# The filter taps as two rounded products over 128 stacked rows in place of one plain product

## The reference, cut to what matters

```python
z = jnp.concatenate([t, jnp.cos(bands * ang), -jnp.sin(bands * ang)], axis=-1)   # 1024 x 33
hid = jnp.sin(fr1 * (z @ w1 + b1))                                               # 1024 x 64
hid = jnp.sin(fr2 * (hid @ w2 + b2))                                             # 1024 x 64
filt = (hid @ w3).reshape(L, HYENA_ORDER, FILTER_DIRS, D_HYENA)                  # 1024 x 2048
filt = filt * jnp.exp(-t * jnp.abs(deltas))[:, None, None, :]
fwd, bwd = filt[:, :, 0], jnp.flip(filt[1:, :, 1], axis=0)
```

## Time and profile before

| | |
|---|---|
| median of 3 runs | 3659.33 us (3657.73 to 3661.23) |
| the profiled execution | 3661.77 us, its span 3660.0 us |
| mean granted clock of TensorE | 0.963 |
| TensorE busy | 3364.4 us (92%), 15224 instructions |
| VectorE busy | 1764.8 us (48%) |
| ScalarE busy | 1115.5 us (30%) |
| GpSimd busy | 579.7 us (16%) |
| the stage of the change | from about 237 to 427 us of the span |

### The profile page before, as it was taken

The page is one execution under the profiler, slowest core; times in us unless marked ns, Lnnn a source line. Parts: engine busy times, 40 slices in busy tenths (PEclk is TensorE's granted clock), DMA queues, the critical chain, the costliest instruction groups (busy, mean ns, idle before and its releaser), DMA issues. The chain is left out here.

```text
span 3660.0 us, 39794 instructions
## 1 busy us (share of the span) xinstructions
PE 3364.4 (92%) x15224; PEld 2696.9 (74%) x15224; DVE 1764.8 (48%) x2726; ACT 1115.5 (30%) x1955; POOL 579.7 (16%) x401
## 2 busy tenths in 40 slices
PE   7999888876989899999999998988899899999998
PEld 5776666665777587888888776776666688888886
DVE  4425544457341435555554539789543423242334
ACT  4323333325232322122111424136675321111212
POOL 0002365642100001010000200000164201000010
PEclk8999999988999999999999999999999999999999
DMA  4232323230321004332221301123233111111111
GB/s 122 75 101 84 118 78 115 87 134 15 117 68 65 37 20 133 98 97 97 97 80 48 133 18 41 46 56 84 67 67 114 39 58 47 46 52 50 47 46 58
DMA packets 223493, 270.27 MB, mean 74 GB/s; under 512 B 17259, under 2 KB 150276, under 8 KB 221298
## 3 DMA queue, kind: packets, MB, share of 16 engines
q1 hardware_dynamic: 223348, 268.30, 23.6%
HBM read 219.68 MB, written 29.18 MB: 68 GB/s over the span
## 5 line engine op out<-in xcount | busy, mean ns | idle before, releaser
L193 PE MATMUL psum<-rounded,rounded 128*128 128x512 f32 (+2 forms) x3936 | 1540.7, 391 | 115.6 <-DVE rounded L222 51.3
L194 PE MATMUL psum<-rounded,rounded 128*128 128x512 f32 (+2 forms) x3936 | 1530.5, 389 | 0.0
L195 PE MATMUL psum<-rounded,rounded 128*128 128x512 f32 (+2 forms) x3936 | 1529.1, 388 | 0.0
L193 PEld LDWEIGHTS psum<-rounded,rounded 128*128 128x128 f32 x3936 | 748.1, 190 | 293.1 <-DVE rounded L222 56.5
L195 PEld LDWEIGHTS psum<-rounded,rounded 128*128 128x128 f32 x3936 | 747.7, 190 | 152.4
L194 PEld LDWEIGHTS psum<-rounded,rounded 128*128 128x128 f32 x3936 | 749.0, 190 | 148.8 <-issue 0.2
L2966 DVE TENSOR_TENSOR plain<-psum,plain 128x512 f32<-128x512 f32 x432 | 288.2, 686 | 110.7 <-PE psum L195 109.1
L2977 DVE TENSOR_TENSOR plain<-psum,plain 128x512 f32<-128x512 f32 x44 | 30.4, 691 | 424.1 <-ACT plain L2881 424.1
L3538 POOL TENSOR_TENSOR plain<-plain,plain 128x128 f32<-128x128 f32 (+3 forms) x64 | 96.9, 1523 | 591.4 <-ACT plain L3636 516.0
L3343 DVE TENSOR_SCALAR_CACHE_REDUCE plain<-plain,plain 128x384 bf16<-128x384 f32 (+2 forms) x204 | 181.8, 942 | 1.3
L2958 DVE TENSOR_TENSOR rounded<-plain,rounded 128x512 fp32r<-128x512 f32 x108 | 97.2, 900 | 164.8 <-ACT rounded L2870 164.6
(11 more groups left out here) (327 smaller groups left out, 3467.1 us busy)
## 6 DMA issues: line engine op xcount, KB each, us to landing
plain<-in_ff_w_dram SPq DMA_DIRECT2D x64, 512.0 KB, 5.4
plain<-in_w_ada_dram SPq DMA_DIRECT2D x96, 256.0 KB, 3.3
plain<-in_w_gu_dram SPq DMA_DIRECT2D x44, 512.0 KB, 4.9
plain<-in_w_in_dram SPq DMA_DIRECT2D x36, 512.0 KB, 4.0
rounded<-rounded SPq DMA_DIRECT2D x72, 256.0 KB, 3.4
plain<-in_c_fwd_dram SPq DMA_DIRECT2D x64, 256.0 KB, 2.6
plain<-in_w_down_dram SPq DMA_DIRECT2D x22, 512.0 KB, 3.7
fold<-plain SPq DMA_DIRECT2D x8, 1024.0 KB, 5.0
```

The costliest lines, as they stand in the source:

```text
L193: nc.tensor.matmul(out, wh, xh, start=first, stop=False)
L194: nc.tensor.matmul(out, wh, xl, start=False, stop=False)
L195: return nc.tensor.matmul(out, wl, xh, start=False, stop=last)
```

## The change

The hidden values are made twice: `w2`, the bias and the frequency are loaded into both halves of the partitions, so that the second hidden layer gives the same 64 channels on partitions 0 to 63 and 64 to 127. A tile `stack` then holds the rounded part of the hidden values in rows 0 to 63 and, after a subtraction, the rest in rows 64 to 127. `w3` is loaded twice too, and `w3_hi` holds its rounded part in all 128 rows, `w3_lo` its rest in 64. A product over the 128 rows gives hi x hi + lo x hi, a second one over 64 rows adds hi x lo. So each plain product becomes two rounded ones.

```diff
-        self.loads = [(self.z, core.ap["c_z"]), (self.w1, core.ap["hy_filt_w1"][0]), (self.w2, core.ap["hy_filt_w2"][0])]
-        for i, name in enumerate(("hy_filt_b1", "hy_filt_freq1", "hy_filt_b2", "hy_filt_freq2")):
-            self.loads.append((self.vec[:, i:i + 1], core.ap[name].rearrange("a c -> c a")))
+        self.loads = [(self.z, core.ap["c_z"]), (self.w1, core.ap["hy_filt_w1"][0])]
+        for part in range(2):
+            rows = slice(64 * part, 64 * part + 64)
+            self.loads.append((self.w2[:, rows], core.ap["hy_filt_w2"][0]))
+            for i, name in enumerate(("hy_filt_b1", "hy_filt_freq1", "hy_filt_b2", "hy_filt_freq2")):
+                self.loads.append((self.vec[rows, i:i + 1], core.ap[name].rearrange("a c -> c a")))
...
     def next_taps(self, sp):
         S = self.core.sig
         sp.wait_ge(S["tap_done"].sem, S["tap_done"].at(8))
-        sp.dma_start(self.w3, self.core.ap["hy_filt_w3"][0][:, L:2 * L]).then_inc(S["taps_loaded"].sem, 16)
+        for rows in (slice(0, 64), slice(64, P)):
+            sp.dma_start(self.w3[rows, :], self.core.ap["hy_filt_w3"][0][:, L:2 * L]).then_inc(S["taps_loaded"].sem, 16)
...
-            last = nc.tensor.matmul(ps[0:64, 6 + half, :], w, x[:, half * BANK:(half + 1) * BANK], start=True, stop=True)
+            last = nc.tensor.matmul(ps[0:64 * (layer + 1), 6 + half, :], w, x[:, half * BANK:(half + 1) * BANK], start=True, stop=True)
...
+    def high(self, act):
+
+        S = self.core.sig
+        act.wait_ge(S["sine_done"].sem, S["sine_done"].at(2))
+        self.core.nc.scalar.activation(self.stack, self.hid, ACT.Copy).then_inc(S["hid_hi"].sem, 1)
+
+    def low(self, dve):
+        S = self.core.sig
+        dve.wait_ge(S["hid_hi"].sem, S["hid_hi"].at(1))
+        self.core.nc.vector.tensor_tensor(self.stack[64:P, :], self.hid[64:P, :], self.stack[64:P, :].bitcast(F32), ALU.subtract).then_inc(S["hid_ready"].sem, 1)
+
+    def taps_high(self, act, o):
+        S = self.core.sig
+        act.wait_ge(S["taps_loaded"].sem, S["taps_loaded"].at(32 * (o + 1)))
+        if o == 0:
+            act.wait_ge(S["mats_rounded"].sem, S["mats_rounded"].at(1))
+        else:
+
+            act.wait_ge(S["tap_done"].sem, S["tap_done"].at(8))
+        self.core.nc.scalar.activation(self.w3_hi, self.w3, ACT.Copy).then_inc(S["taps_hi"].sem, 1)
+
+    def taps_low(self, dve, o):
+        S = self.core.sig
+        dve.wait_ge(S["taps_hi"].sem, S["taps_hi"].at(o + 1))
+        self.core.nc.vector.tensor_tensor(self.w3_lo, self.w3[0:64, :], self.w3_hi[0:64, :].bitcast(F32), ALU.subtract).then_inc(S["taps_lo"].sem, 1)
...
         if n == 0:
-            pe.wait_ge(S["sine_done"].sem, S["sine_done"].at(2))
+            pe.wait_ge(S["hid_ready"].sem, S["hid_ready"].at(1))
         else:
             pe.wait_ge(S["windowed"].sem, S["windowed"].at(n))
         if j == 0 and m == 0:
-            pe.wait_ge(S["taps_loaded"].sem, S["taps_loaded"].at(16 * (o + 1)))
+            pe.wait_ge(S["taps_lo"].sem, S["taps_lo"].at(o + 1))
+        tokens = slice(t * P, (t + 1) * P)
         for half in range(2):
-            last = nc.tensor.matmul(ps[:, 6 + half, :], self.hid[:, t * P:(t + 1) * P], self.w3[:, half * DH:(half + 1) * DH], start=True, stop=True)
+            cols = slice(half * DH, (half + 1) * DH)
+            nc.tensor.matmul(ps[:, 6 + half, :], self.stack[:, tokens], self.w3_hi[:, cols], start=True, stop=False)
+            last = nc.tensor.matmul(ps[:, 6 + half, :], self.stack[0:64, tokens], self.w3_lo[:, cols], start=False, stop=True)
         last.then_inc(S["tap_done"].sem, 1)
...
+                if n == F0:
+                    filters.high(act)
+                    filters.taps_high(act, 0)
...
+                if f == 4:
+                    filters.taps_high(act, 1)
...
+                if n == F0:
+                    filters.low(dve)
+                    filters.taps_low(dve, 0)
...
+                if f == 4:
+                    filters.taps_low(dve, 1)
```

More of the change, by code:

```diff
@@ L664, in hidden @@
         for half in range(2):
-            last = nc.tensor.matmul(ps[0:64, 6 + half, :], w, x[:, half * BANK:(half + 1) * BANK], start=True, stop=True)
+            last = nc.tensor.matmul(ps[0:64 * (layer + 1), 6 + half, :], w, x[:, half * BANK:(half + 1) * BANK], start=True, stop=True)
         last.then_inc(S["hidden_done"].sem, 1)
     def wrapped(self, dve, layer):
-        nc, S, vec = self.core.nc, self.core.sig, self.vec
+        nc, S, rows = self.core.nc, self.core.sig, slice(0, 64 * (layer + 1))
+        vec = self.vec[rows, :]
         chain = Chain(dve, S["wrap_chain"])
@@ L676, in wrapped @@
         dve.wait_ge(S["hidden_done"].sem, S["hidden_done"].at(layer + 1))
-        src = self.core.psum[0:64, 6:8, :].rearrange("p a b -> p (a b)")
+        src = self.core.psum[rows, 6:8, :].rearrange("p a b -> p (a b)")
         if layer == 1:
             dve.wait_ge(S["sine_done"].sem, S["sine_done"].at(1))
-        y, n = self.y, self.n
+        y, n = self.y[rows, :], self.n[rows, :]
         chain(nc.vector.tensor_scalar(y, src, fr, fb, ALU.mult, ALU.add))
@@ L696, in round @@
         act.wait_ge(S["mats_loaded"].sem, S["mats_loaded"].at(16))
-        self.core.nc.scalar.activation(self.rounded, self.mats, ACT.Copy)
+        self.core.nc.scalar.activation(self.rounded, self.mats, ACT.Copy).then_inc(S["mats_rounded"].sem, 1)
     def taps(self, pe, f, m):
@@ L767, in close @@
         S["filter_loaded"].close(16 * len(self.loads))
-        for n, count in (("mats_loaded", 16), ("taps_loaded", 32), ("delta_loaded", 16), ("hidden_done", 2), ("wrap_chain", 12), ("wrap_done", 2), ("sine_done", 2),
+        for n, count in (("mats_loaded", 16), ("taps_loaded", 64), ("mats_rounded", 1), ("hid_hi", 1), ("hid_ready", 1), ("taps_hi", 2), ("taps_lo", 2), ("delta_loaded", 16), ("hidden_done", 2), ("wrap_chain", 12), ("wrap_done", 2), ("sine_done", 2),
                          ("tap_done", 16), ("decay_ready", 16), ("windowed", 16), ("pair_summed", 16), ("pool_chain", 2), ("fold_chain", 8), ("pair_folded", 8), ("fold_stored", 128)):
```

15 lines of the change are left out of this document (8 added, 7 removed).

## The result

The changed kernel takes 3666.64 us, the median of 17 runs (3662.91 to 3671.61); the kernel before, in the same comparison, 3662.37 us (17 runs, 3657.15 to 3667.61). The ratio is 1.0014, with the interval 1.0007 to 1.002: some 5 us slower, a difference whose interval leaves out no change, and that is smaller than the 0.2% I had called no change. I had forecast 5.0 us faster, and the time lies outside the range. The distance to 3654.3 is 12.3 us and has two parts. The base was low by 2.4 us: the three runs shown first have a median of 3659.33, and the many later runs of the same kernel lie around 3661.8, where its profiled execution was. The rest, 10 us, is the step from a gain of 5 to a loss of 5.

A forecast was written before the change was run, and what follows sets the result against it. TensorE was taken to bound the stage. Savings of 3.2 us between halves and 2.25 behind the transposes, less 0.5 for late taps, gave 5.0 us off 3659.33: 3654.3 us, range 3646 to 3661.

The forecast's parts named there:

- The piece: One of 16 tap pieces on TensorE: four rounded products and four row-count changes of 0.20 us, 1.71 us instead of 2.11.
- The saving of 0.40 a piece: Eight pieces between the halves of a tile, where TensorE meets no other engine's wait: 0.40 us each, 3.2 us off.
- the two waits of 1.36: TensorE's waits for VectorE's decay product in the two cycles with extra fold copies: to grow to about 1.8 us.
- The late taps: Ninth piece: the second taps' doubled load, conversion and subtraction make TensorE wait 0 to 0.9 us, taken as 0.5.
- The added loads: Five more first loads on the SP queue at the stage's start: counted as nothing, 0.6 us as the bound.
- the slack of 0.37: Pieces behind the transposes: TensorE comes 0.37 us after VectorE's decay product releases it, so five cycles gain 0.37 each.
- The late cycle: The cycle of the ninth piece, where the second taps arrive late: its saving reduced by the 0.5 us wait.
- What of it reaches the end: The prediction's step on savings reaching the end: 3.2 us between halves, 2.25 behind the transposes, nothing in two long-wait cycles.
- all later stages unmoved: Sign of the forecast: the stage 5 us shorter, later stages unchanged; over 1 us difference in any would contradict it.
- Free changes: Rival: row-count changes cost nothing between rounded products, piece 0.91 us, 12.6 us less, 3646.7 us; chance 0.16.
- The dearer changes: Rival: 0.25 us a row-count change, piece 1.91 us, with late taps 0.9 and first loads 0.6: 3658.0 us; chance 0.14.
- the full drain: Rival: each row-count change drains the array and exposes a weight load, 0.35 to 0.50 us: 3663.0 to 3671.4; chance 0.08.

The follow-up runs named there:

- r10: The kernel before with only the five added first loads and the second hidden layer on 128 partitions: 3661.86 us, ratio 0.9998.
- r5: The changed kernel with seven unused rounded products in each of TensorE's two long waits for the decay product: 3659.53 us, ratio 0.9997.
- r15: The changed kernel with unused products in both long waits (seven each) and in the wait at the ninth piece (three): 3662.55 us, ratio 0.9999.
- r2: The changed kernel with VectorE's fold placed behind the next pair's decay product: 3657.43 us, ratio 0.9987.
- r1: The changed kernel run again without any edit: 3664.99 us, ratio 1.0007 to the kernel before.
- r13: The changed kernel without the second half of the taps, the first half used for all eight pairs: 3664.65 us, ratio 1.0006.
- r4: The kernel before with one more row copy on VectorE ahead of each of the two long folds, lengthening TensorE's waits: 3665.17 us, ratio 1.001.
- r7: The changed kernel with the second product of each half also over all 128 rows, so the row count never changes: 3657.85 us, ratio 0.9988.
- r11: The kernel before with the taps' conversions, doubled loads and waits, and one plain product per half over the rounded parts: 3668.64 us, ratio 1.0018.
- r9: The kernel before run against itself, without any edit: 3663.33 us, ratio 1.0002.
- r14: The kernel before with five unused rounded products in each of its two waits of 1.36 us: 3662.31 us, ratio 0.9997.
- r17: The kernel before with seven unused products (1.6 us) between the halves of tile 3, moving all that follows: 3666.14 us, ratio 1.0008.
- r18: The kernel before with fifteen unused products (3.4 us) between the halves of tile 3, moving all that follows: 3665.82 us, ratio 1.0009.
- r8: The changed kernel with 128 rows in every tap product and VectorE's fold behind the next decay product: 3644.05 us, ratio 0.9951.
- r16: The kernel before with the taps' conversions, doubled loads and one plain product per half, plus three unused products in the ninth piece's wait: 3667.62 us, ratio 1.0014.
- r6: The changed kernel with all its preparation, but one plain product per half over the rounded parts in 64 rows: 3668.18 us, ratio 1.0017.
- r12: A repeat of the changed kernel with one plain 64-row product per half over the rounded parts: 3666.93 us, ratio 1.0017.
- r3: The kernel before with VectorE's fold placed behind the next pair's decay product: 3660.72 us, ratio 0.9999.

## Why the prediction was wrong

*What held.* The piece: 1.71 forecast, 1.70 measured, with 0.20 a change; the steps 0.43 apart. The saving of 0.40 a piece where TensorE doesn't wait, and the two waits of 1.36 that would grow to 1.8: they are 1.77. The late taps: 0 to 0.9 forecast, 0.5 taken, 0.61 measured. The added loads at nothing: r10 shows nothing. The sum for the work in the stage: -5.0 forecast, -3.8 measured.

*The sum's smaller miss.* In four cycles I had counted 0.77 (0.40 and the slack of 0.37) and the trace shows 0.54. The second piece of the pair, between the halves, now meets a wait of about 0.15 us (up to 0.1 forecast), and its first step is 0.42 instead of 0.32. The slack was there, but I spent all of it and let nothing go for the arrival. It is 4 x 0.23 = 0.9 us. The late cycle, with a gain of 0.27 forecast and 0.01 measured, gives the other 0.3.

*The step that failed* is in "What of it reaches the end": "in the two where the fold has its extra copies and TensorE already waits 1.36, nothing", and with it "all later stages unmoved". I priced the two cycles as if the freed 0.4 us only became idle time, and the sum has no term for TensorE's clock. The 0.4 us did become idle time, and behind the two waits TensorE ran at 1.2 GHz for 3.4 and 6.8 us in the changed kernel's profile and lost 1.7 and 3.2 us, 4.9 against a saving in work of 3.8. From 427 to 600 us, where nothing is edited, another 2.2 us went at a granted clock of 0.90 in place of 0.93. I had read the granted clock of 1.00 and the 0.963 of the whole run, seen the waits, and never asked what the clock does if a wait grows or moves. r5 and r15 (idle time filled: clock at 1.00, stage some 3.3 us shorter) and r2 (no waits: the full gain in the stage) show that the stage loses this time only with the array idle in those waits; the profiles of the change, of r1 and of r13 show both drops. That it is the growth of the waits from 1.36 to 1.77 us which brings the drops is not shown: r4 has none behind 1.69 us and r7 none behind 2.58, while r11 has one behind 1.36. The Trainium skill's page TensorE: Matmul & The Clock Gate, A second HAM failure mode, tells of a kernel with cycling PSUM banks, where TensorE's brief idling between groups of products made its clock swing between the two levels; the 1.77 us waits and the stretches at 0.50 behind them agree in that, and r7 and r4 show that here not every such idling was followed by a drop. I hadn't brought it in.

*The rivals.* None was it. Free changes are excluded by the timelines. The dearer changes (3658.0) ended nearer to the measured time, and the full drain (3663.0 to 3671.4) even holds it between its two prices, by a mechanism that isn't there: the piece is 1.70 us, not 2.31 or more. I had written that a difference in a later stage would make the prediction wrong in a way I had no row for; it did.

*What stays open.* Behind the stage the change loses another 2 to 4 us. r9, r10 and r14, which leave the length of the stage as it was, lie within 1 us of before by the means. Most of the others come out 2 to 4 us above what the stage says, r7 6 us, gains and losses alike; r17 and r18 come out at what it says. In the profiles a part of this has a place, the column "next": from 427 to 600 us the change, r1 to r8, r10 to r13, r15 and r16 lose 0.7 to 3.1 us, most of them with less of the upper clock. I had thought that later idle times cost more or less as they fall earlier or later, by the length of the stage. The profiles don't bear that out: r10's loses 2.7 us there with the stage as long as before, and r17's and r18's, whose stages end 3.1 and 3.4 us later, lose none. So it stays open what decides the clock there. Behind 600 us the profiles go apart by -3.1 to +3.7 us, either way. Nor is it settled why the runs of r11 are 5.7 us slower, when its profile shows 2.3.

## What to carry to other kernels

Before costing a shorter operation at its own price, look at what TensorE does with the time: if it goes into a wait that is already there, TensorE only stands idle for longer, and a lower clock behind such a wait can cost more than was saved (4.9 us against 3.8 here, in one profile). Shorten what the wait is for first, or with it (here VectorE's order, one exchange of two calls), and only then the products: the changed kernel with both edits (r8) is 18 us below the kernel before, with either alone (r2, r7) some 5. And a product that mixes row counts can lose to one that computes more rows than it needs: the piece took 1.70 us with 64 rows in every second product and 0.91 with 128 in all.

## What the runs showed of the hardware

- A change between 128 and 64 contraction rows costs 0.20 us a change also between rounded products: steps of 0.43 against 0.227 (the change against r8).
- Idle times of TensorE as short as 1.36 to 1.77 us were followed by stretches of 3.4 to 6.8 us at a granted clock of 0.50. The length of the wait didn't decide it: none of the four waits of 1.69 us (r4) and 2.58 us (r7) was followed by one, all six of 1.77 us (the change, r1, r13) were, and of the 18 of 1.34 to 1.36 us five (r6, r11, r12, r16, r17). How long the lower clock then lasts varies with the same code (r1 against the first profile), and a shift of 1.6 us with the same wait came with a drop (r17). With products in the idle time (r5, r14, r15) or without idle time (r2, r3, r8) none was seen behind these pieces.
- At the lower level the changed piece's steps are 0.72 us and those of the rounded products 0.43, from 381.31 on in the timeline above: both the product and the change of row count become slower.
- Most edits of the stage came with a longer stretch from 427 to 600 us, by 0.7 to 3.1 us, whichever sign they had in the stage, and most with less of the upper clock there (0.90 in the changed kernel, r4 and r10, 0.93 before). A shift of all that follows by 1.6 or 3.4 us alone (r17, r18) didn't.
